# Key half groups one pair ahead of the heads, the samples' softmax beside the last pair, and a third buffer for selected values

## What is computed

```python
def dense_gqa(q, k, v, dist, valid):
    s = jnp.einsum('...tkgd,...skd->...kgts', q, k).astype(jnp.float32) * HEAD_DIM ** -0.5
    s = s - alibi_slopes()[:, :, None, None] * dist[..., None, None, :, :]
    p = masked_softmax(s, valid[..., None, None, :, :])
    o = jnp.einsum('...kgts,...skd->...tkgd', p.astype(v.dtype), v)
    return o, p
```

## Time and profile before

| What | Value |
|---|---|
| median of 3 runs | 3568.38 us (3568.25 to 3568.88) |
| profiled execution, its own time | 3566.33 us |
| its span, first to last instruction | 3564.8 us |
| PE busy | 3249.1 us (91%) |
| DVE, ACT, POOL busy | 1789.6, 1227.0, 337.5 us |
| mean granted PE clock | 0.954 |

### The profile page before, as it was taken

The page is one execution under the profiler, slowest core; times in us unless marked ns, Lnnn a source line. Parts: engine busy times, 40 slices in busy tenths (PEclk is TensorE's granted clock), DMA queues, the critical chain, the costliest instruction groups (busy, mean ns, idle before and its releaser), DMA issues. The chain is left out here.

```text
span 3564.8 us, 56642 instructions
## 1 busy us (share of the span) xinstructions
PE 3249.1 (91%) x21882; PEld 2921.2 (82%) x21882; DVE 1789.6 (50%) x2615; ACT 1227.0 (34%) x1508; POOL 337.5 (9%) x536
## 2 busy tenths in 40 slices
PE   6999899669799999999979998986697999999998
PEld 4776777449799999999957767764597999999998
DVE  4887465633433333444448974656233333334443
ACT  2212363323333333333322124533233333333333
POOL 0002132330100000000000021323301000000000
PEclk8999999779999999999989999998899999999999
DMA  4326454664344444444332273646733444444443
GB/s 157 121 95 244 157 180 166 212 239 159 124 161 164 162 163 159 158 164 165 118 121 101 102 268 126 212 157 196 253 143 118 165 165 165 165 165 165 165 164 122
DMA packets 143638, 579.67 MB, mean 163 GB/s; under 512 B 21009, under 2 KB 92850, under 8 KB 117746
## 3 DMA queue, kind: packets, MB, share of 16 engines
q1 hardware_dynamic: 106706, 491.89, 37.7%
q0 software_dynamic: 24672, 71.07, 5.9%
q10 hardware_dynamic: 12096, 14.69, 1.2%
HBM read 570.02 MB, written 24.18 MB: 167 GB/s over the span
## 5 line engine op out<-in xcount | busy, mean ns | idle before, releaser
L1003 PE MATMUL banks<-normed_hi,weights_hi 128*128 128x288 f32 x4736 | 1408.6, 297 | 55.8 <-POOL normed_lo L537 34.1
L1003 PE MATMUL banks<-normed_lo,weights_hi 128*128 128x288 f32 x4736 | 1400.3, 296 | 0.0
L1003 PE MATMUL banks<-normed_hi,weights_lo 128*128 128x288 f32 x4736 | 1395.6, 295 | 0.0
L1359 DVE TENSOR_TENSOR weights_lo<-weight_slots,weights_hi 128x2048 fp32r<-128x2048 f32 x296 | 680.6, 2299 | 1104.9 <-ACTq L1284 1104.9
L1281 ACT ACTIVATE weights_hi<-weight_slots 128x2048 fp32r<-128x2048 f32 x296 | 567.0, 1916 | 1143.9 <-PE banks L1003 1136.1
L1003 PEld LDWEIGHTS banks<-normed_hi,weights_hi 128*128 128x128 f32 x4736 | 890.8, 188 | 58.3 <-issue 55.4
L1003 PEld LDWEIGHTS banks<-normed_hi,weights_lo 128*128 128x128 f32 x4736 | 895.1, 189 | 0.0
L1003 PEld LDWEIGHTS banks<-normed_lo,weights_hi 128*128 128x128 f32 x4736 | 892.3, 188 | 0.6
L632 PE MATMUL banks<-normed,weight_slots 128*128 128x288 f32 x1664 | 438.4, 414 | 0.0
L632 PEld LDWEIGHTS banks<-normed,weight_slots 128*128 128x128 f32 x1664 | 321.7, 194 | 92.6 <-issue 2.8
L808 PE MATMUL banks<-conv_high,conv_weights 128*128 128x508 f32 x1024 | 332.4, 406 | 19.7 <-DVE conv_low_a L1359 10.8
(11 more groups left out here) (273 smaller groups left out, 2489.0 us busy)
## 6 DMA issues: line engine op xcount, KB each, us to landing
weight_slots<-in_w_gu SPq DMA_DIRECT2D x88, 2048.0 KB, 7.7
weight_slots<-in_w_down SPq DMA_DIRECT2D x44, 2048.0 KB, 7.7
weight_slots<-in_w_in SPq DMA_DIRECT2D x28, 2048.0 KB, 7.9
arena<-in_cache_cmp SPq DMA_DIRECT2D x256, 128.0 KB, 4.1
arena<-in_cache_cmp POOLq DMA_DIRECT2D x256, 128.0 KB, 4.3
weight_slots<-in_w_out SPq DMA_DIRECT2D x16, 2048.0 KB, 7.8
arena<-in_cache_slc_k SPq DMA_DIRECT2D x128, 128.0 KB, 3.1
arena<-in_cache_slc_k POOLq DMA_DIRECT2D x128, 128.0 KB, 3.5
```

The costliest lines, as they stand in the source:

```text
L1003: mm = pe.matmul(out, wt[:, hf, col], x[:, rhs + c, :], start=begin and c == 0 and i == 0, stop=hf == 1 and c == k - 1 and i == 2, skip_gr ...
L1359: return dve.tensor_tensor(out, a, b, op)
```

## The change

Keys: on PE and DVE the half groups go ahead by up to a pair. On PE the scores of heads 0 and 1 now come before the window's second half group, and the eight half groups stand before `turn_and_weigh(0)` (0,0; 0,1), in it (1,0), before and in `turn_and_weigh(1)` (1,1; 2,0; 2,1), before and in `turn_and_weigh(2)` (3,0; 3,1). The last pair has no key work. Samples' softmax: `sw_max` comes before the last pair's scaling; ACT takes SW's exponential before the last pair's copies and SS's after them; the last pair's two `weigh` stand in the sets of turned samples, before the fourth. Values: three page buffers in the order 0, 2, 1, 0, 2, 1, 0, 1 for b = 0 to 7 (0 is the ring, 1 is `a_s`, 2 is slot 1, where the heads' buffers lay); buffer 2 waits for `po_done` 8, the last `weigh`. Samples 0 and 1 are split 8 and 8 on SP and POOL, and ACT issues none of them; the other six stay 6, 5, 5. SP loads row 0 of the output projection after sample 0's values, and row 1 once sample 4 is through with slot 1.

```diff
+    vbufs = [a_ring, a_s, WR[:, 1, :, :].rearrange("p a b -> p (a b)")]
+    VB = [0, 2, 1, 0, 2, 1, 0, 1]
+    VW = [a_qp[:, 1024 * i:1024 * i + 1024] for i in range(2)]
+    def value_parts(b):
+        return {"full": range(0, NPG, 2), "more": range(1, NPG, 2)} if b < 2 else \
+            {part: range(i, NPG, 3) for i, part in enumerate(("full", "more", "rest"))}
...
-                eng.wait_ge(*((S["st_done"], 12) if hb else (S["kring_free"], 22)))
+                last = [c for c in range(b) if VB[c] == VB[b]][-1:]
+                if not last:
+                    eng.wait_ge(*((S["kring_free"], 22), (S["st_done"], 12), (S["po_done"], NQ))[VB[b]])
                 for x, page in zip(mine, p):
-                    eng.wait_ge(S["vring_free"], b * 5 + x // 4 + 1)
+                    for c in last:
+                        eng.wait_ge(S["vring_free"], 10 + 5 * c + x // 4 + 1)
...
-                slot_load(J_OUT, slot(0), row("w_out", lay * 8))
...
+                for b in range(NB):
+                    values(sp, b, "full")
+                    sp.wait_ge(S["kring_free"], 22)
+                    sp.wait_ge(S["vring_free"], b * 5 + 5)
+                    sp.dma_start(VW[b % 2], row("win_v", lay * NB + b)).then_inc(S[f"vwin{b % 2}_full"], 16)
+                    if b == 0:
+                        slot_load(J_OUT, slot(0), row("w_out", lay * 8))
+                sp.wait_ge(S["vring_free"], 34)
...
-                for e in range(2):
-                    keys(1, e, 128)
...
+                def turn_and_weigh(i, between=()):
+                    n = 2 * i
                     turn_p(n, a)
+                    for x in between[:1]:
+                        half_group(*x)
                     turn_p(n + 1, b_)
+                    for x in between[1:]:
+                        half_group(*x)
                     weigh(n, a, n // GQA)
                     weigh(n + 1, b_, n // GQA)
+
+                for e in range(2):
+                    keys(1, e, 128)
+                half_group(0, 0)
+                mask()
+                half_group(0, 1)
+                scores(2, a, 0)
+                scores(3, b_, 0)
+                turn_and_weigh(0, ((1, 0),))
+                half_group(1, 1)
+                scores(4, a, 1)
+                scores(5, b_, 1)
+                turn_and_weigh(1, ((2, 0), (2, 1)))
+                half_group(3, 0)
+                scores(6, a, 1)
+                scores(7, b_, 1)
+                turn_and_weigh(2, ((3, 1),))
+                turn_p(6, a)
+                turn_p(7, b_)
...
+                    if i == 3:
+                        weigh(6, a, 1)
+                        weigh(7, b_, 1)
+                        pe.wait_ge(S["sw_ready"], 3)
...
+                act.wait_ge(S["sw_max"], 1)
+                sample_exp(1, SW)
+                for j, h in enumerate(HEADS):
+                    turned(6 + j, h)
+                sample_exp(0, SS)
...
+                window_out(1)
+                dve.tensor_reduce(mxw[:, :, 0], SW[:, :, 0:WIN], AXX, ALU.max)
+                dve.wait_ge(S["tables_back"], 16)
+                keys_out(0, 0)
...
+                prompt_scale(2, a)
+                prompt_scale(3, b_)
+                keys_out(1, 1)
+                prompt_bias(4, a)
+                prompt_bias(5, b_)
+                keys_out(2, 0)
+                keys_out(2, 1)
+                masked(1)
+                prompt_out(2)
+
+                prompt_scale(4, a)
+                prompt_scale(5, b_)
+                keys_out(3, 0)
+                prompt_bias(6, a)
+                prompt_bias(7, b_)
+                keys_out(3, 1)
+                masked(2)
+                masked(3)
+                prompt_out(4)
                 dve.drain()
                 dve.tensor_reduce(SM[:, 54:56], mxs, AXX, ALU.max)
                 dve.tensor_reduce(SM[:, 56:58], mxw, AXX, ALU.max)
                 dve.drain()
                 dve.tensor_scalar(SM[:, 54:58], SM[:, 54:58], -1.0, None, ALU.mult).then_inc(S["sw_max"], 1)
+                prompt_scale(6, a)
+                prompt_scale(7, b_)
...
+                    if i == 0:
+                        prompt_out(6)
                     dve.drain().then_inc(S["sw_ready"], 1)
```

More of the change, by code:

```diff
@@ L314, in conv_pages, with values @@
                                           .rearrange("a p x -> p (a x)")).then_inc(S[f"raw{u % 2}_{sem}"], 16)
[L316 to L320, removed]
-                eng.wait_ge(*((S["st_done"], 12) if hb else (S["kring_free"], 22)))
+            def values(eng, b, part):
+                mine = value_parts(b)[part]
+                before = sum(len(value_parts(b)[x]) for x in list(value_parts(b))[:list(value_parts(b)).index(part)])
+                p = page_list(eng, (2 * NB + b) * NPG + before, len(mine))
+                sem = "more" if part == "more" else "full"
+                last = [c for c in range(b) if VB[c] == VB[b]][-1:]
+                if not last:
+                    eng.wait_ge(*((S["kring_free"], 22), (S["st_done"], 12), (S["po_done"], NQ))[VB[b]])
                 for x, page in zip(mine, p):
-                    eng.wait_ge(S["vring_free"], b * 5 + x // 4 + 1)
-                    eng.dma_start(vbufs[hb][0][:, 256 * x:256 * x + 256],
+                    for c in last:
+                        eng.wait_ge(S["vring_free"], 10 + 5 * c + x // 4 + 1)
+                    eng.dma_start(vbufs[VB[b]][:, 256 * x:256 * x + 256],
                                   T["cache_slc_v"][bass.ds(lay * 160 + page, 1)].rearrange("a p x -> p (a x)"))\
-                        .then_inc(S[f"vbuf{hb}_{part}"], 16)
+                        .then_inc(S[f"vbuf{VB[b]}_{sem}"], 16)
             def swapped(v):
@@ L529, in _ @@
                             key_pages(pool, i, hf, e, "more")
-                for i in range(NB // 2):
-                    for hb in range(2):
-                        values(pool, i, hb, "more")
+                for b in range(NB):
+                    values(pool, b, "more")
                 for n in range(8):
@@ L967, in _ @@
                         if n == 0:
-                            for part, c in (("full", 96), ("more", 80), ("rest", 80)):
-                                pe.wait_ge(S[f"vbuf{hb}_{part}"], i * c + c)
+                            pe.wait_ge(S[f"vbuf{VB[b]}_full"], value_count(b, "full"))
+                            pe.wait_ge(S[f"vbuf{VB[b]}_more"], value_count(b, "more"))
                         if n == 4:
@@ L1229, in _, with turned, sample_exp @@
                     prompt_exp(j, h)
[L1230 to L1242, removed]
+                def turned(n, h):
+                    act.wait_ge(S["pt_done"], n + 3)
+                    act.activation(h.pt[:, 0:4, :].rearrange("p n s -> p (n s)"), bank(6), ACT.Copy)
+                    act.activation(h.pt[:, 4:6, :].rearrange("p n s -> p (n s)"), bank(7)[:, 0:256], ACT.Copy)
+                    act.activation(h.ptc, bank(7)[0:NCMP_P, 256:512], ACT.Copy)
+                    act.drain().then_inc(S["pt_evac"], 1)
+                def sample_exp(i, v):
                     for k in range(NKV):
@@ L1656, in _, with window_out @@
                 dve.drain()
-                for hf in range(2):
+                def window_out(hf):
                     dve.wait_ge(S["kring_free"], 2 * hf + 4)
@@ L1887, in arrays_of @@
     a["pages"] = np.concatenate([pages.reshape(-1), pages.reshape(4, 2, 4, 2, 2).transpose(2, 3, 4, 1, 0).reshape(-1),
-                                 pages[:, [x for part in range(3) for x in range(part, NPG, 3)]].reshape(-1)])[None, :]
+                                 pages[:2, [x for part in range(2) for x in range(part, NPG, 2)]].reshape(-1),
+                                 pages[2:, [x for part in range(3) for x in range(part, NPG, 3)]].reshape(-1)])[None, :]
     a["w_in"] = blocks(v["w_in"][:, :, :NTILE * P], KC, 256)
```

93 lines of the change are left out of this document (40 added, 53 removed).

## The result

The changed kernel takes 3554.68 us (median, 3548.58 to 3561.68), the kernel before 3568.32 in the same runs. The ratio is 0.9964, 95% interval 0.9956 to 0.9973: 13.6 us faster, half of the 26 forecast. The profiled execution has a span of 3552.3 us and took 3553.86.

The account below looks back on a forecast made before the run. In attention, a chain of waits was taken to bound the key half and DMA bandwidth the value half. Earlier keys and value stream, less softmax costs, gave 13 us a layer, 26 for both: median 3542, range 3526 to 3562.

Parts of the forecast that it names:

- likeliest case: The forecast itself: faster, median 3542 us, own range 3529 to 3552, chance 0.56.
- rival (c): Third buffer comes too late to be one; stream starts 4.5 us earlier only: 9 us for both layers, 3559; chance 0.19.
- C: Segment from a layer's first value matmul to the end of the last sample: forecast 5.5 us shorter.
- Part 1: Key chain to half group (3,1): seven steps of 8.5 us, ending at 687.1, 12.2 us earlier.
- Part 2: From the last key part to the maxima (`sw_max`): 11.2 us instead of 9.7, giving back 1.5 us.
- Part 3: Samples' softmax beside the last pair: fourth set at 713.2, 4.2 us earlier; costs 6.5 us of the 10.7.
- Part 4: Turning and copying, fourth set to first value matmul: 7 us instead of 10.3; first value matmul 7.5 us earlier.
- B: Segment from the end of half group (3,1) to the first value matmul: forecast 4.7 us longer.
- Part 5: Value stream: sample 1 at 712.5, 11.6 us earlier; third buffer gives 1.4 us; last sample ends 13 us earlier.
- Sum: All terms together: 13 us a layer, 26 for both layers, median 3542.
- A: Segment from a layer's first compressed-score matmul to the end of half group (3,1): forecast 12.2 us shorter.
- (d): Slower: PE stands at a key part while a head is ready; gain gone at 10.4 us a step; chance 0.11.

## Why the prediction was right or wrong

The likeliest case, faster, was right in its sign, and the time is inside the range and outside the likeliest case's own (3529 to 3552). Nearest in time is rival (c), 3559, though not by its mechanism: the third buffer does come late, but still takes 4 us a layer off C, and what is missing is missing in the key half.

**Part 1 failed: "(3,1) ends at 627.6 + 7 * 8.5 = 687.1, 12.2 earlier".** This is the term that was mis-sized, and wrongly shared out. In four layers of the change (3,1) ends at 88.8, 92.4, 89.6 and 92.9, 7.7 earlier than the 98.6 of before. By the prediction's own sign (a last key part after 692, which is 90.6 us into a layer) Part 1 is wrong in the second layer of both profiles and not in the first. Nearly all of the 7.7 needs no new order: with the 2 MB moved and the old order, the ten layers of five runs have 91.0 to 94.7, mean 92.7; the eight layers of the four runs with the new order and the 2 MB moved have 88.8 to 94.8, mean 92.1. The order is worth 0.6 us there, too little to be told from nothing with layers that spread over 4 to 6 us, and I had given it 8.5 (12.2 less the 3.7 of the 2 MB). The two don't add: the order alone gives 5.5, the 2 MB alone 6.4, both 7.7.

Why didn't a step come down to 8.5? The four layers of the change have 62.6 to 66.7 us for seven steps, 9.2 each. I had named the tight place, (1,1) to (2,1), at 14.1 us by the heads' work and 17.0 by two steps. It took 655.47 to 672.92 = 17.45 in the first layer and 19.2 in the second. Pages are the smaller part of that: in the run of the change without key loads the stretch still takes 650.41 to 667.38 = 17.0 us, and 17.0 in its second layer. Its rows of (1,1), (2,0) and (2,1):

```profile
648.47 1.94 PE L856 MATMUL banks<-arena 128*32 128x256 f32 x32
...
656.66 1.94 PE L856 MATMUL banks<-arena 128*32 128x256 f32 x32 [1.71 <-DVEq L1751]
...
663.74 3.64 PE L856 MATMUL banks<-arena 128*32 128x256 f32 x32 [4.12 <-DVEq L1751]
```

So the heads' work is 17.0 here, and my 14.1 for it was 2.9 short. It left out the 1.71 us in which PE waits, ahead of (2,0), for DVE to take out (1,1), which stands behind two scalings on DVE's list; with pages to load, a wait of 1.73 us for them in the middle of (2,0) is there in its place. And the stop of some 4.1 us ahead of (2,1), which I had in the sum, has a price behind it. In the changed kernel the 32 matmuls then take 3.96 us instead of 2.12, since they begin at a granted clock of 0.50 (1.2 GHz) after the stop, where the x32 row at 687.69, with PE busy before it, has 1.00 (2.4 GHz). The two stretches, in the columns of the earlier trace rows:

```profile
668.90:672.90 4.00, 3.84 (x33) 1.42 (x33) 0.00 (x0) 2.17 (x12) 1.22 (x3) 0.50 0.35 109
687.60:689.80 2.20, 2.20 (x35) 0.89 (x34) 1.86 (x4) 1.11 (x3) 0.00 (x0) 1.00 0.11 38
```

In DVE's rows the stop is visible as a circle: the bias of head 5 waits for `turn_p(3)` (2.45 us), which stands behind half group (2,0) on PE; the next half group's release (L1643) stands behind that bias.

```profile
665.29 1.14 DVE L1717 SCALAR_TENSOR_TENSOR weight_slots<-consts,banks 128x512 f32<-128x512 f32 x2 [2.45 <-PE banks L897]
...
667.84 0.17 DVE L1727 TENSOR_SCALAR smalls<-smalls 128x6 f32<-128x6 f32 x1
667.92 0.86 DVE L1643 SCALAR_TENSOR_TENSOR arena<-consts,banks 128x256 f32<-128x256 f32 x2
672.98 0.87 DVE L1643 SCALAR_TENSOR_TENSOR arena<-consts,banks 128x256 f32<-128x256 f32 x2 [4.20 <-PE banks L858]
```

A second reason is read from the trace, not tried by a run: when PE is late and takes both parts at once (the x32 rows at 623.64 and 668.96), both come free together, and POOL refills them one behind the other:

```profile
671.57 2.31 POOL L316 DMA_DIRECT2D arena<-in_cache_slc_k  x4 [4.77 <-PE banks L858]
674.30 2.31 POOL L316 DMA_DIRECT2D arena<-in_cache_slc_k  x4 [0.42 <-issue]
```

Part e = 1 then costs 0.67 + 2.31 + 0.42 + 2.31 + 3.6 + 1.07 = 10.4 from the moment part 0 is free, 1.07 of it beside part 1's own matmuls: 9.3 a step, an estimate. The steps agree in direction: in the first layer the two behind these rows take 10.4 and 9.5 us, the other five 7.4 to 9.5, 8.5 in the mean, which is what I had for all. I had named this, and let it move my choice only between 7.7 and 9.0.

So both bounds that I took the larger of were too small. That the page loads hold the steps up is shown by the run without them, where a step of the new order takes 7.8 us for 9.2; how the 1.4 divides between pages that land late and pages that are issued one behind the other is open.

**Part 2 was right**: 689.8 to 700.9 is 11.1 us, forecast 11.2. **Part 3 was right too**: fourth set 15.6 us behind `sw_max` (14.9 forecast), at 716.50 instead of 713.2, of which 2.6 come from Part 1 and 0.7 are its own. **Part 4 was exact** in its size: 7.0 us from the fourth set to the first value matmul. The three together, B, were forecast at 33.1 and are 34.3 in the mean of four layers; the rest is 1.2. One term in Part 3 is a slip: 8.4 us by the share 2080 of 2624 is 6.7, not 6.4. It changes nothing, since the other branch was the longer.

But what they say together I did not draw out. Parts 2 and 3 put 11.2 + 14.9 us behind the last key because the head steps that the keys had overtaken are done there: `prompt_bias(7)`, two maskings, `prompt_out(4)`, the scalings. DVE's path to the maxima behind (3,1) is 11.1 us in the change and 4.3 under the old key order with the same softmax (693.97 to 698.2 in that run's profile). Keys put ahead of heads on two engines that keep the order of their lists left the heads' work behind the last key. The wait on DVE itself is no longer than it was, 8.02 us at 702.92 against 7.67 in the kernel before:

```profile
712.74 2.37 PE L937 MATMUL banks<-consts,arena 128*128 128x128 f32 x10 [7.67 <-DVEq L1762]
```

But there all heads were weighed before it, and in the change the last pair is still to be turned and weighed behind it. I booked the 6.5 us against the softmax; by the table it belongs to the key order.

**Part 5** was right in size, at 343 GB/s for 59 us: C was to fall by 5.5 and fell by 5.0. That is in part luck. Rival (c) puts the layer without an early third buffer at 4.5 us gained for 13, so the forecast had 8.5 a layer on that buffer, and the run with two buffers shows 4. Sample 1 starts at 715.45 instead of 712.5, 2.7 of it Part 1's. Row 0 costs nothing there, as costed: it is issued 20 us ahead of sample 1, and a 2 MB row lands 7.7 us after its issue (median of the page).

**Sum**: of the 6.5 us a layer that are missing, 4.5 are A's, 1.2 B's and 0.5 C's; the rest is rounding. Of the rivals, (d) is nearest in mechanism: keys ahead of heads hold the heads up, and alone, the order is slower than before, 1.0021. But its price was wrong too. It asked for steps above 10.4 us; they are 9.2, and the loss lies behind the last key, in B. I gave it 0.11 because I compared its step with the 10.2 of before, and the long last step in that 10.2 belonged to the 2 MB.

The ledger by ratios, of 3568 us, each part on top of those before it: the 2 MB moved -9.6; samples 0 and 1 off ACT's queue and split 8 and 8 -13.2; the third buffer -5.5; keys a pair ahead, with the softmax beside the last pair, +16.4. Sum -11.9, the mean of the two measurements of the change.

## What to carry to other kernels

Before an order is changed to shorten a chain of loads, take out the one foreign load that lies beside it, and measure: here 2 MB made the last step 12.2 us long where it is 8.5 without them, and moving them is one line. Work that is put ahead of other work on an engine that keeps its list's order has to be charged with what it leaves behind the new end of the chain; read the time from the last key to the next stage, not only the time to the last key. And a list of DMA issues on an engine that also copies for the critical path is worth more than it looks: five page loads away from ACT, with the split they allow, brought as much as the whole change. And a bound that is worked out from rows (14.1 us for the heads) can be measured by a run that takes the other bound away (17.0).

## What the runs showed of the hardware

In the stretch with sample 0's pages and the 2 MB together, the changed kernel's DMA engines moved 400 GB/s for 8 us, and the value half 341 GB/s for 50 us at a DMA share of 1.00:

```profile
694.50:702.50 8.00, 0.40 (x2) 0.00 (x1) 7.41 (x19) 3.92 (x16) 0.91 (x2) 0.70 1.05 400
720.00:770.00 50.00, 37.84 (x698) 28.15 (x700) 11.01 (x25) 11.82 (x25) 16.68 (x32) 0.86 1.00 341
```

The prediction cited the Trainium skill (DMA: Bandwidth & Descriptors, section "Specifications") for a limit of about 358 GB/s. The page stream agrees with it, the 8 us with the large load don't. Even divided by their share of 1.05 they are 381 GB/s. So full DMA engines with 128 KB pages and 512 KB window values moved less than full engines with a 2 MB load among them, and the page stream was the slower of the two by 15% (10% if both are taken at a share of 1.00).

A layer's key half varies by 2 to 4 us between layers and runs of one kernel (88.8 to 92.9 for the change), and from 91.0 to 94.7 over the five runs with the old order and the 2 MB moved, which is as much as the effects argued about. It took several kernels with the same part to see that the order was worth about nothing there.
